# Attention with pairwise normalisation: reciprocals of two heads in one instruction, one head part and the conv products moved in the order

## The reference, cut to what matters

```
a = u[..., :C] * sigmoid(u[..., C:])             # 512 channels
a = depthwise_conv(a, 31 taps) + conv_b
a = silu(layernorm(a) * g + b)

q, k = rotary(rms(...))                          # 8 heads of 96
s = q @ k.T                                      # per head, 1024 x 1024
p = softmax(s)
att = p @ v                                      # 8 heads of 64
mix = concat([a, att]) @ w_out
```

## Time and profile before

| | us |
|---|---|
| median of three runs | 1939.68 |
| profiled execution | 1936.98 |
| its span (first to last instruction) | 1935.2 |
| PE busy | 1849.0 (96%) |
| DVE busy | 1400.9 (72%) |
| ACT busy | 798.7 (41%) |
| POOL busy | 794.4 (41%) |

### The profile page before, as it was taken

The page is one execution under the profiler, slowest core; times in us unless marked ns, Lnnn a source line. Parts: engine busy times, 40 slices in busy tenths (PEclk is TensorE's granted clock), DMA queues, the critical chain, the costliest instruction groups (busy, mean ns, idle before and its releaser), DMA issues.

```text
span 1935.2 us, 22706 instructions
## 1 busy us (share of the span) xinstructions
PE 1849.0 (96%) x8035; PEld 1467.1 (76%) x8035; DVE 1400.9 (72%) x1814; ACT 798.7 (41%) x1248; POOL 794.4 (41%) x601
## 2 busy tenths in 40 slices
PE   4999999999999999997999998999999999999997
PEld 3787778778888878985565565877888888888886
DVE  6678888986777785776788877358656555677778
ACT  4532232223344554236676643154323323234453
POOL 1076655665200010017999942013666656620000
PEclk9999999999999999997999999999999999999999
DMA  9046666544763351000000014112332323466333
GB/s 348 13 141 195 208 206 203 194 158 172 257 218 99 111 182 63 10 1 1 1 1 1 0 55 152 63 63 82 115 109 96 116 88 109 169 235 237 94 109 125
DMA packets 132797, 232.12 MB, mean 120 GB/s; under 512 B 8781, under 2 KB 66228, under 8 KB 132435
## 3 DMA queue, kind: packets, MB, share of 16 engines
q1 hardware_dynamic: 132500, 230.73, 35.1%
q10 hardware_dynamic: 190, 0.01, 0.0%
HBM read 177.75 MB, written 52.95 MB: 119 GB/s over the span
## 4 chain that ended last, share of the span: by engine, by line
PE 38%; DVE 10%; POOL 2%; issue 2%; ACT 1%; DMA 1%; DVEq 0%; POOLq 0%; ACTq 0%
PE ps L502 18%; PE ps L854 9%; PE ps L2751 4%; PE ps L1658 2%; DVE cv L1828 2%; DVE negmax L1595 1%; PE ps L1636 1%; DVE grow L1674 1%; PE ps L376 1%; POOL cv L1818 1%; PE ps L1587 1%; PE ps L1711 1%; DVE T L935 0%; PE ps L1609 0%; POOL wor L1914 0%
## 5 line engine op out<-in xcount | busy, mean ns | idle before, releaser
L502 PE MATMUL ps<-T,ring 128*128 128x512 f32 x1920 | 441.8, 390 | 0.0
L502 PEld LDWEIGHTS ps<-T,ring 128*128 128x128 f32 x1920 | 360.6, 188 | 74.8 <-DVE ring L479 0.2
L502 PE MATMUL ps<-B,ring 128*128 128x512 f32 x1440 | 344.9, 396 | 2.2 <-DVE SG L561 2.2
L502 PEld LDWEIGHTS ps<-B,ring 128*128 128x128 f32 x1440 | 271.9, 189 | 66.5 <-issue 10.7
L954 POOL TENSOR_SCALAR stat<-stat 128x1 f32<-128x1 f32 x32 | 10.7, 334 | 549.2 <-ACT XS L879 259.7
L568 POOL TENSOR_TENSOR HID<-HID,SG 128x512 f32<-128x512 f32 x80 | 119.5, 1493 | 265.2 <-DVE HID L553 152.6
L854 PE MATMUL ps<-PW 128*128 128x512 f32 x924 | 217.3, 390 | 0.0
L854 PE MATMUL ps<-PT 128*128 128x512 f32 x900 | 212.1, 390 | 0.0
L854 PEld LDWEIGHTS ps<-PW 128*128 128x128 f32 x924 | 173.4, 188 | 35.9
L854 PEld LDWEIGHTS ps<-PT 128*128 128x128 f32 x900 | 168.6, 188 | 34.7
L479 DVE TENSOR_TENSOR ring<-sums,ring 128x512 fp32r<-128x512 f32 x160 | 159.5, 1008 | 45.7 <-ACT ring L473 45.7
(11 more groups left out here) (336 smaller groups left out, 3306.9 us busy)
## 6 DMA issues: line engine op xcount, KB each, us to landing
adat<-ffn_hidden SPq DMA_DIRECT2D x154, 256.0 KB, 2.7
ada_raw<-in_w_ada SPq DMA_DIRECT2D x56, 512.0 KB, 3.9
rawg<-in_ffn_wg SPq DMA_DIRECT2D x22, 1024.0 KB, 5.4
rawu<-in_ffn_wu SPq DMA_DIRECT2D x22, 1024.0 KB, 5.2
ffn_hidden<-HID SPq DMA_DIRECT2D x84, 256.0 KB, 2.6
ffn_hidden<-base SPq DMA_DIRECT2D x66, 256.0 KB, 2.6
H<-in_x SPq DMA_DIRECT2D x16, 512.0 KB, 6.6
h_saved_rows<-H SPq DMA_DIRECT2D x16, 512.0 KB, 2.6
```

Of the source, the lines that this page charges most:

```text
L502: mm = e.matmul(ps[:, product_bank(M, k)], ring[:, place % RING, wx, kc], RIGHT[k][:, xx, kc], start=(kc == 0 and i == 0), stop=(kc == HC ...
```

## The change

Three things are done at once.

- ACT copies the outputs and the sums of a finished unit with two instructions of 64 partitions instead of one of 128: the outputs to `grow`, the sums to `tmp`, both on the partitions of their head (0 to 63 for the first, 64 to 127 for the second) and in the columns of their query half. When both heads of a query half are there, DVE takes the reciprocals of both in three instructions on 128 partitions and scales both with one. There are six reciprocals and two multiplications in a turn instead of twelve and four. They stand in A units and at the start of unit 1.
- The fourth part of the next head (second half of its queries) is transposed in step 0 of the B unit, behind `pe_max`, instead of in step 3 of the A unit. The row at the end of an A unit waits for one part fewer (7 for 8). The tap of step 0 in B goes to the end of the A unit, behind the row's low part.
- ACT makes the product of step 3 ahead of its copy of the row instead of behind the exponential.

```diff
@@ pe_max_row
-            e.wait_ge(qk_lo, 3 if first else i * 8 + (4 * (m // NH) + (8 if ahead else 4)))
+            e.wait_ge(qk_lo, 3 if first else i * 8 + (4 * (m // NH) + (7 if ahead else 4)))
@@ act_pv_copy and the normalisation
+            hp, h = (m - 1) % NU // NH, (m - 1) % NH
             e.wait_ge(pv_mm, i * 4 + m)
-            if not (isinstance(i, int) and i == 0 and m == 1):
-                e.wait_ge(pv_out, i * 4 + (m - 1))
-            e.activation(grow[:, 0:HALF], ps[:, 6], ACT.Copy).then_inc(pv_copied, 1)
+            if hp == 0 and not (isinstance(i, int) and i == 0):
+                e.wait_ge(pv_out, i * NH + (h - 1))
+            of = slice(hp * VH, (hp + 1) * VH)
+            e.activation(grow[of, h * HALF:(h + 1) * HALF], ps[0:VH, 6], ACT.Copy)
+            e.activation(tmp[of, h], ps[VH:2 * VH, 6], ACT.Copy).then_inc(pv_copied, 1)
...
-            e.reciprocal(grow[0:VH, HALF + a:HALF + b], grow[VH:2 * VH, a:b]).then_inc(pv_rec, 1)
+            e.reciprocal(tmp[:, h, a:b], tmp[:, h, a:b]).then_inc(pv_rec, 1)
...
-            e.tensor_tensor(dst, grow[0:VH, 0:HALF], grow[0:VH, HALF:D], ALU.mult).then_inc(pv_out, 1)
+            dst = att[:, bass.ds(i - 1, 1), h * HALF:(h + 1) * HALF].rearrange("p a q -> p (a q)")
+            e.tensor_tensor(dst, grow[:, h * HALF:(h + 1) * HALF], tmp[:, h], ALU.mult).then_inc(pv_out, 1)
@@ pe_turn_head
                 if n == 0:
                     e.wait_ge(m_lo, i * 4 + (hp * 2 - 1))
+                elif n == 3:
+                    e.wait_ge(m_lo, i * 4 + hp * 2)
@@
+        HEAD_AT = {(0, 0): 0, (0, 1): 1, (0, 2): 2, (1, 0): 3}
@@ unit of ACT
-                    if m % NH == 0 and not (last and m // NH == 1):
-                        act_head_unit(e, *next_head(i, m), p)
+                    if (m % NH, p) in HEAD_AT and not (last and m // NH == 1):
+                        act_head_unit(e, *next_head(i, m), HEAD_AT[m % NH, p])
+                    if p == 3 and not last:
+                        for n in products(m, p, p + 1):
+                            act_prod(e, i, n, first)
                     if p == 3 and not (last and m == NU - 1):
                         act_max_hi(e, i, m + 1)
...
-                    if not last:
+                    if p < 3 and not last:
                         for n in products(m, p, p + 1):
                             act_prod(e, i, n, first)
@@ unit of DVE
+                    if not first:
+                        if m == 0 and p > 0:
+                            dve_pair_recip(e, i, 0, p - 1)
+                        elif (m, p) == (1, 0):
+                            dve_pair_scale(e, i, 0)
+                        elif m == 2 and p < 3 and not (last and p == 2):
+                            dve_pair_recip(e, i, 1, p)
+                        if (m, p) == ((2, 3) if last else (2, 2)):
+                            dve_pair_scale(e, i, 1)
+                    if (m % NH, p) == (0, 3) and not last:
+                        dve_tap(e, i * DTT + (DT + m // NH * 2), (0,))
@@ unit of PE
-                    if m % NH == 0 and not (last and m // NH == 1):
+                    if m % NH == 0 and p < 3 and not (last and m // NH == 1):
                         pe_turn_head(e, *next_head(i, m), p)
                     if not (last and m == NU - 1):
                         pe_max(e, i, m + 1, p)
+                    if m % NH == 1 and p == 0 and not (last and m // NH == 1):
+                        pe_turn_head(e, *next_head(i, m), 3)
```

More of the change, by code:

```diff
@@ L2516, in unit @@
                         dve_max(e, i, m + 1, p)
-                    if m % NH == 0:
+                    if (m % NH, p) in HEAD_AT:
                         if not (last and m // NH == 1):
-                            dve_head_unit(e, *next_head(i, m), p)
-                    elif not last:
+                            dve_head_unit(e, *next_head(i, m), HEAD_AT[m % NH, p])
+                    elif m % NH == 1 and not last:
                         dve_tap(e, i * DTT + (DT + m // NH * 2 + p // 2), (p % 2,))
-                    if last and m == 2 and p == 3:
-                        dve_pv_recip(e, *at(i, m - 1), 2)
+                    if last and (m, p) == (2, 3):
+                        dve_pair_recip(e, i, 1, 2)
                     if p == 3 and not (last and m == NU - 1):
@@ L2530, in unit @@
                         dve_ln_var(e)
-                    if not (first and m < 2):
-                        if p == 3:
-                            dve_pv_scale(e, *at(i, m - 1))
-                        elif not (last and m == 2 and p == 2):
-                            dve_pv_recip(e, *at(i, m - 1), p)
+                    if not first:
[9 more added lines that the diff above has]
+                        dve_tap(e, i * DTT + (DT + m // NH * 2), (0,))
                     if last and m == 1 and p in (1, 2):
@@ L2551, in cut_mix @@
                 if t == 0 and part == 1:
-                    e.wait_ge(pv_out, NU * TURNS)
+                    e.wait_ge(pv_out, NH * TURNS)
                 if t >= 2:
@@ L2563, in _ @@
             for third in range(3):
-                dve_pv_recip(e, TURNS, -1, third)
-            dve_pv_scale(e, TURNS, -1)
+                dve_pair_recip(e, TURNS, 0, third)
+            dve_pair_scale(e, TURNS, 0)
             cut_mix(0, 0)
@@ L2568, in _ @@
             for third in range(3):
-                dve_pv_recip(e, TURNS, 0, third)
-            dve_pv_scale(e, TURNS, 0)
+                dve_pair_recip(e, TURNS, 1, third)
+            dve_pair_scale(e, TURNS, 1)
             cut_mix(0, 1)
```

11 lines of the change are left out of this document (4 added, 7 removed).

## The result

| | before | after |
|---|---|---|
| median of the runs | 1939.68 us (1936.99 to 1942.16, 5 runs) | 1959.16 us (1951.75 to 1960.07, 5 runs) |
| profiled execution, its span | 1936.98, 1935.2 us | 1959.47, 1957.7 us |
| turns 0 to 2 in the profile | 206.7 us | 228.2 us |
| turn 3 in the profile | 72.2 us | 72.2 us |
| from the last looped turn's end to the last instruction | 833.4 us | 833.7 us |

The changed kernel is slower: ratio 1.0089, 95% interval 1.0077 to 1.01 (the two medians alone give 1.0100; the ratios here are not quotients of medians). The forecast was 1937.7 us with a range of 1929 to 1943.5. The table also says where to look: the first three turns lose 21.5 us, all else nothing. (Turns are counted from row to row: from the first matmul at L1609 that transposes the maxima for a turn's first unit to the same place of the next turn. Turn 0 of before lies at 895.02 to 964.20.)

What follows compares the result with a forecast made beforehand. PE was taken to set the pace, POOL 4.08 us a turn behind it. Terms of 0 (turns 0 to 2), -0.7 (turn 3) and -1.3 (behind the turns) gave -2.0: 1939.68 to 1937.7 us, range 1929 to 1943.5.

Steps and rivals of the forecast that it cites:

- Reciprocals and multiplications: On DVE: 1.15 us per reciprocal on 128 partitions, about 7 us shed a turn, B row some 0.5 us earlier.
- Second copy: On ACT, once per unit: about 0.58 us more work, zero effect in turns 0 to 2, bounds -0.1 and 0.6 per unit.
- Fourth head part: Its transposes (0.39 us) change step: zero as work; the A row starts at about 1015.7 instead of 1016.92.
- Product ahead of the row: On ACT at every unit's end, called the deciding step: sum 0 over turns 0 to 2, bounds -12 and +14 us.
- the two ends: Ends of A and B units, read from timelines: -0.1 us at A, between -0.1 and +0.65 at B.
- I take that to give back the 0.65: Start of B units: POOL, no longer idle for up to 1.4 us, was to make up the B end's +0.65 us.
- The moved tap: Before B's first maximum: meeting an addition it takes 2.41 for some 1.34 us, about 1 us in each of three turns.
- second rival: B ends and starts: low part late behind the third product, POOL held by DVE's tap; +4.9, about 1944.6 us; chance 0.13.
- Turn 3 and behind the turns: Turn 3: -0.7 us, bounds -2.2 and +0.6. Behind the turns, earlier scaling and output projection: -1.3, bounds -1.8 and 0.
- Signs I named: Trace features listed beforehand as showing the forecast right, with a turn of 68 to 70 us, or wrong.
- above 70 (second): Sign that the forecast is wrong: a turn above 70 us points to the second rival.

Runs made afterwards that it cites:

- e9: Kernel before with only the paired reciprocals and multiplications and the second copy; transposes, taps and product unmoved: 1938.24 us, ratio 1.0001.
- e4: Changed kernel with the moved tap back in step 0 of B and the product back behind the exponential: 1930.08 us, ratio 0.9947.
- e2: Changed kernel with the moved tap put ahead of the reciprocal at the end of the A unit instead of behind it: 1949.26 us, ratio 1.0043.
- e3: Changed kernel with only the product of step 3 put back behind the exponential: 1936.96 us, ratio 0.9982.
- e12: Changed kernel with four product buffers in place of two, nothing moved: 1938.12 us, ratio 1.0002.
- e5: Kernel before with only the last product of each unit put ahead of the row's copy on ACT: 1954.07 us, ratio 1.0071.
- e6: Changed kernel with POOL's three slot instructions of a B unit put behind that unit's first product: 1979.70 us, ratio 1.02.
- e11: Changed kernel with the moved tap in step 2 of the A unit and the product back behind the exponential: 1941.41 us, ratio 1.001.
- e13: e4 with four product buffers in place of two: 1932.32 us, ratio 0.9968.

## Why the prediction was wrong, step by step

- **Reciprocals and multiplications**: priced 1.15 us on 128 partitions, measured 1.14; worth nothing in a looped turn beyond the room on DVE (e9: 68.72 for 68.73). I had expected the B row some 0.5 us sooner; in e9's turn 2 the B units are 15.99 and 15.92 for 15.99 and 16.07. Right in cost, and nearly so in effect.
- **Second copy**: 0.59 as priced.
- **Fourth head part**: "zero as work", with the earlier row counted only together with the product. The row does start behind the last maximum. Alone the move is worth 1.4 us a looped turn (e9 to e4), which the forecast had hidden by adding the product to it: what the head part gains, the product takes. The better sum prices each edit alone, with the others undone.
- **Product ahead of the row**, "Sum over the twelve units of turns 0 to 2: 0": the step that failed. The three turns took 21.5 us more. The reading of the two ends was near: from the row to the transposes at a B end it is 0.64 more (3.80 for 3.16) where I had +0.65, and the A units of turn 1 are 0.5 and 0.4 shorter where I had 0.1. What failed first is "I take that to give back the 0.65". In e2's turn 1, with nothing shut out, the B units are 1.4 and 0.5 longer than before, more than the A units are shorter, and the turn is 1.0 longer (69.77 against 68.80). It is 3.0 longer than with the product back (e3), and I had compared only with before. The second failure is a mechanism I didn't see, and it has most of the loss: by keeping POOL supplied the product closed the gaps through which DVE's two-input instructions got in. I had counted a POOL that is never idle as pure gain.
- **The moved tap** (second rival), "takes 2.41 for some 1.34 and stands in front of the first maximum, about 1 us in each of three turns": the right place and the right pair of instructions, but a price of 1.07 from a row in which the tap had started 0.1 us before one addition ended and got in when the next one did. Measured 6.49, 5.32 and 5.33 us, then an idle PE and half its clock: against e2's undisturbed 17.3, unit 1 of turns 1 and 2 lost 6.1 and 5.7 us, and in turn 0, where no such kernel is at hand, 7.6 against the 18.09 of e12. That is about 19.4 us (6.1 + 5.7 + 7.6) of the 21.5, an estimate for turn 0's part. The rule of the Trainium skill (SBUF — State Buffer, "SBUF: two separate sides") agrees with the traces in that the two lock each other out for the length of an instruction (here 5.32 us of waiting and working for the tap); who follows when the holder ends it does not say, and I took for granted that it would be the one that waits.
- **Turn 3 and behind the turns**: forecast -0.7 and -1.3, measured -0.3 for turn 3 (its first three units -0.59, -0.27, +0.61) and -0.4 from there to the output projection (31.18 us for 31.56). The mechanism (scaling early, then ACT's activation as the wait) was right; the slow four products at 1195.26 cost 1.5 us. In e4 and e9, where they took 1.88, the stretch is 29.5 and 29.6 us: -2.0, more than forecast. In the changed kernel the rest of the program was then 0.9 us longer, inside what identical code spreads by, so nothing of the -2.0 is left in its profile.
- **Signs I named**: ACT's wait before the last product, the row behind the maximum, the copy more than 1.5 us behind the row, the scaling straight behind w_out were all there. The turn "above 70 (second)" was the sign of the second rival, and it came.

Which cause is shown: the product ahead of the row, by e3 and e4 (22 and 20 us back) and by e5, where it alone costs 15. That it acts through the ring of two buffers is shown by e12 (waits gone, 21 us back) and by e6. That the victim need not be the tap is shown by e5. The late copy and the shutting out hang together, since the same product makes both, and e12's trace is free of both, so it doesn't divide them. Nor is the product needed for a dense chain: the nine cases of shutting out in looped turns are all in kernels with the product ahead, but three of the seven in turn 0 (5.96 us in e4, 3.54 in e11, 4.97 in e13) are in kernels with it behind. What is not settled is what decides, of two like instructions in like places, which is let in: in the changed kernel the tap that started 0.08 us into an addition lost at each of the next three ends, and in e2 the one that started 0.25 us into one won at the first; but in e5 one that started 0.25 into it lost four times. So the 20 us could not have been forecast to the microsecond from the rows of before. The runs of one kernel spread, too: the changed one by 8 us over 5 runs, e12 by 20 over 12, before by 8 over 23; that they do so for this reason is likely and not shown.

## What to carry to other kernels

Before work is put ahead of something urgent on an engine's queue, ask what that work itself waits for: behind a ring of two buffers, everything after it inherits the other engine's delay. An engine that is fed more steadily is not only a gain: where instructions of two engines shut each other out, as DVE's and POOL's did here, its gaps were someone's way in, and the upper bound to put down for a collision is the whole unbroken run of the other side, not one instruction. Price each edit alone, since a gain and a loss that stand in one sum hide each other.

## What the runs showed of the hardware

A DVE instruction with two SBUF inputs that starts while POOL is in a chain without gaps is not sure of its turn at the next end of a POOL instruction. Over the looped and first turns of the 14 traces I count 16 such instructions that had been waiting for over 0.3 us when a POOL instruction ended, and still did not get in; they took 2.95 to 6.50 us; 15 of these ran through POOL's three slot instructions (L1764, L1766, L1770; L1762, L1764, L1768 in the old numbering), and one, of 3.45 us in e6, through two additions. While they were kept out, POOL's instructions had their plain lengths (1.05, 0.62, 1.48). Where they got in, it was POOL's next instruction that was longer by about a microsecond (2.25 for 1.27).

PE's clock: in the changed kernel, after an idle time of 3.81 us, the granted clock was 0.50 for the next stretch (1001.80 to 1007.00), the 1.2 GHz level, and 1.00 again in the unit after. A wait of about 2 us went either way. In turn 3, 13 of the 14 traces have PE waiting 1.78 to 2.22 us for an exponential ahead of the same scores. The four products behind them took 1.88 us in six (after 2.21 us of waiting in the kernel before) and 2.28 to 3.52 in seven (3.39 after 2.11 in the changed kernel). What tips it is not shown.
